# A trunk kernel whose last down projection streams 512 weight columns per matmul, with ten constant matmuls behind each post-norm sum

## What is computed

```
for i in range(DEPTH):
    y = swiglu(rms_norm(h, g[0]), ffn_w_gate[i, 0], ffn_w_up[i, 0], ffn_w_down[i, 0])
    h = h + 0.5 * rms_norm(y, g[1])
    u = rms_norm(h, g[2])
    y = mixer_ab(u, ...) if i % 2 == 0 else mixer_cd(u, ...)
    h = h + rms_norm(y, g[3])
    y = swiglu(rms_norm(h, g[4]), ffn_w_gate[i, 1], ffn_w_up[i, 1], ffn_w_down[i, 1])
    h = h + 0.5 * rms_norm(y, g[5])
return h[:, N_META:]
```

## Time and profile before

| | |
|---|---|
| median of three runs | 1197.17 us (1193.57 to 1197.82) |
| profiled execution | 1195.76 us |
| its span, first to last instruction | 1193.8 us |
| PE busy | 1138.9 us, 95% |
| DVE busy, ACT busy | 714.5 us, 547.3 us |
| mean granted TensorE clock | 0.978 |

### The profile page before, as it was taken

How to read it: one execution, slowest core, us unless ns; L and a number is a source line. 1 busy time by engine, 2 the same in 40 slices (tenths; PEclk the granted TensorE clock), 3 DMA queues, 4 the chain that set the end, 5 groups by cost and what they waited for, 6 DMA issues and landing times.

```text
span 1193.8 us, 20098 instructions
## 1 busy us (share of the span) xinstructions
PE 1138.9 (95%) x8979; PEld 1113.5 (93%) x8979; DVE 714.5 (60%) x753; ACT 547.3 (46%) x623; POOL 8.7 (1%) x12
## 2 busy tenths in 40 slices
PE   5999999899999899999999999999899699999997
PEld 5999999789999789999998999999899498999996
DVE  5565644668784676656446656554757636756542
ACT  5534343456633565343434544344463545444441
POOL 0000000000000000000000000000001100000000
PEclk9999999899999999999999999999999789999998
DMA  8656557677432145555563655455264024555530
GB/s 253 189 170 195 168 173 164 129 154 139 91 107 71 36 142 181 174 177 167 167 195 106 212 177 177 164 164 176 90 218 130 1 88 156 181 178 189 177 128 36
DMA packets 175780, 178.70 MB, mean 150 GB/s; under 512 B 4912, under 2 KB 174400, under 8 KB 175696
## 3 DMA queue, kind: packets, MB, share of 16 engines
q1 hardware_dynamic: 175696, 177.44, 49.8%
HBM read 176.38 MB, written 1.05 MB: 149 GB/s over the span
## 4 chain that ended last, share of the span: by engine, by line
PE 90%; DVE 5%; ACT 2%; DMA 2%; issue 1%; SPq 0%; DVEq 0%; ACTq 0%
PE ps L1531 24%; PE ps L1533 24%; PE ps L1532 24%; PE ps L1601 8%; PE ps L1568 2%; PE ps L1596 2%; PE ps L1569 2%; PE ps L1565 2%; DMA raw<-ab_w_in 1%; DVE w_lo L1018 1%; DVE hT L1067 1%; DVE yT L1066 1%; ACT w_hi L631 0%; DMA g_tok<-norm_gains 0%; PE ps L1588 0%
## 5 line engine op out<-in xcount | busy, mean ns | idle before, releaser
L1531 PE MATMUL ps<-u_hi,w_hi 128*128 128x272 f32 (+1 forms) x1696 | 491.3, 290 | 0.0
L1533 PE MATMUL ps<-u_hi,w_lo 128*128 128x272 f32 (+1 forms) x1696 | 487.9, 288 | 0.0
L1532 PE MATMUL ps<-u_lo,w_hi 128*128 128x272 f32 (+1 forms) x1696 | 486.0, 287 | 0.0
L1018 DVE TENSOR_TENSOR w_lo<-raw,w_hi 128x2048 fp32r<-128x2048 f32 (+1 forms) x169 | 378.0, 2259 | 123.3 <-ACT w_hi L631 123.3
L631 ACT ACTIVATE w_hi<-raw 128x2048 fp32r<-128x2048 f32 (+1 forms) x169 | 314.8, 1870 | 178.3 <-PE ps L1533 164.5
L1531 PEld LDWEIGHTS ps<-u_hi,w_hi 128*128 128x128 f32 x1696 | 319.5, 188 | 1.8 <-issue 0.8
L1532 PEld LDWEIGHTS ps<-u_lo,w_hi 128*128 128x128 f32 x1696 | 319.4, 188 | 0.3
L1533 PEld LDWEIGHTS ps<-u_hi,w_lo 128*128 128x128 f32 x1696 | 319.4, 188 | 0.0
L1531 PE MATMUL ps<-hid_hi,w_hi 128*128 128x272 f32 (+1 forms) x704 | 201.5, 286 | 0.0
L1533 PE MATMUL ps<-hid_hi,w_lo 128*128 128x272 f32 (+1 forms) x704 | 201.2, 286 | 0.0
L1532 PE MATMUL ps<-hid_lo,w_hi 128*128 128x272 f32 (+1 forms) x704 | 200.9, 285 | 0.0
(11 more groups left out here) (291 smaller groups left out, 939.6 us busy)
## 6 DMA issues: line engine op xcount, KB each, us to landing
raw<-ffn_w_gate SPq DMA_DIRECT2D x44, 1024.0 KB, 5.4
raw<-ffn_w_up SPq DMA_DIRECT2D x44, 1024.0 KB, 5.3
raw<-ffn_w_down SPq DMA_DIRECT2D x32, 896.0 KB, 4.6
raw<-ffn_w_down SPq DMA_DIRECT2D x16, 1024.0 KB, 5.0
raw<-ab_w_in SPq DMA_DIRECT2D x16, 1024.0 KB, 13.7
raw<-cd_w_in SPq DMA_DIRECT2D x9, 1024.0 KB, 5.4
raw<-ab_w_out SPq DMA_DIRECT2D x4, 1024.0 KB, 5.1
raw<-cd_w_out SPq DMA_DIRECT2D x4, 1024.0 KB, 5.1
```

Source lines behind the costliest of these rows:

```text
L1018: dve.tensor_tensor(dst, src, w_hi[:, n % NW, 0:rows(n) * CB].bitcast(F32), ALU.subtract)\
L1531: pe.matmul(o, wh, rhs_hi[:, kk, tok], start=first and kk == 0, stop=False)
L1532: pe.matmul(o, wh, rhs_lo[:, kk, tok], start=False, stop=False)
L1533: ins = pe.matmul(o, wl, rhs_hi[:, kk, tok], start=False, stop=last and kk == rows(n) - 1)
```

## The change

Two things are changed. First, behind `post_norm_sum` of every sub-layer but the last, PE runs ten float32 matmuls of `ones` against `ident`, 128 columns each, into a PSUM bank that nobody reads (`keep_clock`). They wait for nothing.

Second, the down projection of the last sub-layer is written anew (`last_down` on PE, ACT and DVE). The hidden activations become the stationary operand (128 tokens) and the weights the moving one, 512 columns at a time; there are two halves of 512 output features, each with six chunks of 4 or 3 rows (`LAST_ROWS`), and two tiles of 128 tokens, so 2 x 2 x 22 x 3 = 264 matmuls. The result is token-major. `hT` is transposed behind the first chunk and copied to `h_tok`. ACT squares a tile of the result with a sum along its free axis (`accum_out`), DVE adds the two sums of a token tile and multiplies the result by a row of gains (`g_row`, a new load of one row broadcast to 128 partitions), ACT makes the inverse root of one column, and DVE scales and adds `h_tok` in one instruction for each 512 columns. SP stores from `y_tok`, again in four pieces. The final post-norm, `make_input` and transposes of before are gone.

```diff
+LAST_ROWS = ((0, 4), (4, 8), (8, 12), (12, 16), (16, 19), (19, 22))
...
+                    if k == len(subs) - 1:
+                        sp.dma_start(g_row[:, :], a["norm_gains"][layer, norm_of(k) + 1:norm_of(k) + 2, :].to_broadcast([P, D]))\
+                            .then_inc(s_grow, 16)
+                        for z in range(2):
+                            for i, (k0, k1) in enumerate(LAST_ROWS):
+                                load(b + 2 * NPAIR + len(LAST_ROWS) * z + i, wd[:, k0:k1, z * BANK:(z + 1) * BANK], BANK)
+                        continue
...
+            def last_down(f, b):
+
+                n = b + 2 * NPAIR
+                for i in range(2):
+                    hi(n + i + 3)
+                for t in range(2):
+                    for z in range(2):
+                        act.wait_ge(s_hT, 2 * t + z + 1)
+                        act.activation(h_tok[:, t, z * BANK:(z + 1) * BANK], ps[:, 4 + 2 * t + z, :], ACT.Copy)\
+                            .then_inc(s_htok, 1)
+                for z in range(2):
+                    for i in range(len(LAST_ROWS)):
+                        if z or i > 1:
+                            hi(n + len(LAST_ROWS) * z + i + 3)
+                    for t in range(2):
+                        act.wait_ge(s_used, n + len(LAST_ROWS) * (z + 1)) if t else act.wait_ge(s_yt, z + 1)
+                        if z:
+                            act.wait_ge(s_yts, t + 1)
+                        act.activation(y_sq_tok[:, t, :], ps[:, 2 * z + t, :], ACT.Square, accum_out=y_sums[:, t, z:z + 1])\
+                            .then_inc(s_yts, 1)
+                        if z:
+                            act.wait_ge(s_ytot, t + 1)
+                            step.done(act.activation(y_root[:, t:t + 1], y_root[:, t:t + 1], ACT.Ln, bias=EPS, scale=1.0 / D))
+                            act.activation(y_root[:, t:t + 1], y_root[:, t:t + 1], ACT.Exp, bias=LN_HALF, scale=-0.5)\
+                                .then_inc(s_yroot, 1)
...
+            def last_down(f, b):
+
+                n = b + 2 * NPAIR
+                for z in range(2):
+                    cols = slice(z * BANK, (z + 1) * BANK)
+                    for i in range(len(LAST_ROWS)):
+                        lo(n + len(LAST_ROWS) * z + i + 3)
+                    if z == 0:
+                        dve.wait_ge(s_grow, 16)
+                        dve.wait_ge(s_htok, 4)
+                    for t in range(2):
+                        dve.wait_ge(s_yts, 2 * z + t + 1)
+                        if z:
+                            dve.tensor_tensor(y_root[:, t:t + 1], y_sums[:, t, 0:1], y_sums[:, t, 1:2], ALU.add).then_inc(s_ytot, 1)
+                        step.done(dve.tensor_tensor(y_tok[:, t, cols], ps[:, 2 * z + t, :], g_row[:, cols], ALU.mult))
+                        if z:
+                            dve.wait_ge(s_yroot, t + 1)
+                            for x in range(2):
+                                c_ = slice(x * BANK, (x + 1) * BANK)
+                                dve.scalar_tensor_tensor(y_tok[:, t, c_], y_tok[:, t, c_], y_root[:, t:t + 1], h_tok[:, t, c_],
+                                                         ALU.mult, ALU.add).then_inc(s_otok, 1)
...
+            def keep_clock(k):
+
+                bank = {"ffn": 3, "ab": 1, "cd": 3}[subs[k][0]]
+                for _ in range(10):
+                    pe.matmul(ps[:, bank, 0:P], ones[:, :], ident[:, :], start=True, stop=True)
...
+                for z in range(2):
+                    for i, (k0, k1) in enumerate(LAST_ROWS):
+                        n = b + 2 * NPAIR + len(LAST_ROWS) * z + i
+                        pe.wait_ge(s_lo, n + 1)
+                        pe.wait_ge(s_hid, 2 + NPAIR * f + (k1 + 1) // 2)
+                        for t in range(2):
+                            o, tok = ps[:, 2 * z + t, :], slice(N_META + t * P, N_META + (t + 1) * P)
+                            for kk in range(k0, k1):
+                                w = slice((kk - k0) * BANK, (kk - k0 + 1) * BANK)
+                                wh, wl = w_hi[:, n % NW, w], w_lo[:, n % NR, w]
+                                pe.matmul(o, hid_hi[:, kk, tok], wh, start=kk == 0, stop=False, skip_group_check=True)
+                                pe.matmul(o, hid_hi[:, kk, tok], wl, start=False, stop=False, skip_group_check=True)
+                                ins = pe.matmul(o, hid_lo[:, kk, tok], wh, start=False, stop=kk == KF - 1,
+                                                skip_group_check=True)
+                            if t == 0 and k1 == KF:
+                                ins.then_inc(s_yt, 1)
+                        ins.then_inc(s_used, 1)
...
                 post_norm_sum(k)
-
-            for g in range(2):
-                for t in range(2):
-                    pe.wait_ge(s_h, KD * len(subs) + 4 * g + 4)
-                    for m in range(4):
-                        src = hT[:, 4 * g + m, N_META + t * P:N_META + (t + 1) * P]
-                        ins = pe.transpose(ps[:, 2 + 2 * t + g, m * P:(m + 1) * P], src, ident[:, :])
-                    ins.then_inc(s_oT, 1)
+                keep_clock(k)
```

More of the change, by code:

```diff
@@ L310, in build @@
         s_dve = sem("dve_step")
-        s_oT = sem("output_transposed")
-        s_oa = sem("first_output_tile_copied")
-        s_oc = sem("second_output_tile_copied")
+        s_grow = sem("last_gain_row_loaded")
+        s_hT = sem("last_input_transposed")
+        s_htok = sem("last_input_copied")
+        s_yt = sem("last_y_ready")
+        s_yts = sem("last_y_squared")
+        s_ytot = sem("last_y_squares_added")
+        s_yroot = sem("last_y_root_ready")
+        s_otok = sem("output_ready")
         s_out = sem("output_stored")
@@ L472, in rows @@
                 if b <= n < b + SIZES[kind]:
+                    if b + SIZES[kind] == n_chunks and n - b >= 2 * NPAIR:
+                        k0, k1 = LAST_ROWS[(n - b - 2 * NPAIR) % len(LAST_ROWS)]
+                        return 2 * (k1 - k0)
                     if kind == "ffn" and n - b >= 2 * NPAIR:
@@ L525, in _, with load @@
             sp.dma_start(g_tok[:, :], a["norm_gains"].rearrange("l s (m p) -> (l s m) p", p=P)).then_inc(s_in, 16)
-            def load(n, src):
+            def load(n, src, cols=CB):
                 if n >= NR:
                     sp.wait_ge(s_used, n - NR + 1)
-                dst = raw[:, n % NR, 0:rows(n) * CB].rearrange("p (k c) -> p k c", c=CB)
+                dst = raw[:, n % NR, 0:rows(n) * CB].rearrange("p (k c) -> p k c", c=cols)
                 sp.dma_start(dst, src).then_inc(s_raw[n % NR], 16)
@@ L587, in _ @@
                         load(b + CD_CHUNKS + i, w_out[:, :, c0:c0 + CB])
-            for g in range(2):
[L590 to L593, removed]
+            for t in range(2):
+                for z in range(2):
+                    cols = slice(z * BANK, (z + 1) * BANK)
+                    sp.wait_ge(s_otok, 2 * t + z + 1)
+                    sp.dma_start(out[0, t * P:(t + 1) * P, cols], y_tok[:, t, cols]).then_inc(s_out, 16)
             sp.wait_ge(s_out, 64)
@@ L989, in _ @@
                     act.preload_act_table_set(EXP_SET)
+                    if k == len(subs) - 1:
+                        last_down(f, b)
+                        break
                     for blk in range(NBLK):
@@ L999, in _ @@
                 post_norm(k, kind)
-            for g in range(2):
-                act.wait_ge(s_oT, 2 * g + 1)
-                act.activation(o_tok[:, 0, g * BANK:(g + 1) * BANK], ps[:, 2 + g, :], ACT.Copy).then_inc(s_oa, 1)
         @block.vector
@@ L1084, in make_input @@
                         update_h(k, 2 * g + 2, 2 * g + 4)
[L1085 to L1088, removed]
+                    input_lo(k, layer, g)
                 for g in range(1, KD // 2):
@@ L1512, in _ @@
                     cd(k, b)
[L1513 to L1517, removed]
         @block.tensor
@@ L1598, in half_tile, with last_down @@
                 return ins
+            def last_down(f, b):
+                for z in range(2):
+                    for i, (k0, k1) in enumerate(LAST_ROWS):
+                        n = b + 2 * NPAIR + len(LAST_ROWS) * z + i
+                        pe.wait_ge(s_lo, n + 1)
+                        pe.wait_ge(s_hid, 2 + NPAIR * f + (k1 + 1) // 2)
+                        for t in range(2):
+                            o, tok = ps[:, 2 * z + t, :], slice(N_META + t * P, N_META + (t + 1) * P)
[9 more added lines that the diff above has]
+                        ins.then_inc(s_used, 1)
+                        if z == 0 and i == 0:
+                            pe.wait_ge(s_prod, 2 + NPAIR * f + NPAIR)
+                            for t in range(2):
+                                for g in range(2):
+                                    for m in range(4):
+                                        src = hT[:, 4 * g + m, N_META + t * P:N_META + (t + 1) * P]
```

(6 more changed lines are left out.)

10 lines of the change are left out of this document (7 added, 3 removed).

## The result

| | before | after |
|---|---|---|
| median of four runs each | 1196.79 us | 1183.65 us (1182.82 to 1184.62) |
| profiled execution, its span | 1195.76, 1193.8 us | 1184.62, 1182.7 us |
| mean granted clock | 0.978 | 0.983 |

The ratio after to before is 0.9895, with a 95% interval of 0.9874 to 0.9916: 13.1 us by the medians, and faster by more than the 0.5% that can be told. The forecast was 1185.0 us. The two profiled executions differ by 11.1 us; that of after was the slowest of its four runs.

What follows compares the result with a forecast made beforehand. PE bounds the kernel, busy 95% of the span. Clock -5.7, wider matmuls 0, transposes +1.75 and shorter end -7.6 sum to -11.5 us; forecast 1185.0 us, range 1180.5 to 1190.0.

Steps and rivals of the forecast that it cites:

- gap 3: Behind sub-layer 3, DVE and ACT set the pace, so keeping the clock there gains nothing.
- the fillers stay covered: Ten constant matmuls take 2.2 us at full clock and end before the next sub-layer's first matmul; 0.6 us cover left.
- the end of the program: From the last down matmul's end to the span's end: 5.7 us in place of 13.3, so -7.6 us.
- gap 0: Behind sub-layer 0 the ten run slowly and end 0.9 us late, 1.8 us are won back: 0.9 us gained.
- The worth of a fall: Behind sub-layers 1, 2 and 4, keeping full clock saves 1.6 us each, 4.8 us together.
- the wait for the third block of `u_hi`: At full clock PE uses up two blocks before the third comes, losing 0.1 us of the gain again.
- The width of a matmul: Last down projection: excess grows with columns, 512 take 0.2358 us, no gain from width; transposes add 1.75 us.
- the fixed-cost rival: Last down projection: 11.2 ns excess paid per matmul, so halving the matmuls gives 3.0 us more, 1182.0 us; chance 0.2.
- Constants that don't count: Rival: fillers behind the post-norm sums don't keep the clock, it falls as before; 1190.7 us, chance 0.13.
- The slow form of 512 columns: Rival: 512-column matmuls in the last down projection run at another rate; at 0.472 us each, 1247 us; chance 0.03.
- a supply that falls behind: Rival: last stage's weight chunks of other shape arrive late and PE waits up to 5 us; 1190 us, chance 0.04.
- The clock fell no later behind sub-layer 3: Rival: PE at full clock stands still more often between `u_hi` blocks, clock falls later; +1.7 us, 1186.7 us, no chance given.

## Why the prediction was right

**Point by point.** The time lies 1.3 us under the forecast and inside the range. That the clock is held behind 1 to 4, that gap 3 is worth nothing, that the fillers stay covered there (0.3 us of idleness is left in the timeline), and the end of the program, step by step, were right: the end is 5.6 us against 5.7, each step within 0.1 us. That the sum came so near is in part luck. Between the profiles the three falls gave 0.9 us less than forecast and gap 0 0.6 us less, and the last down projection cost 1.3 us less, so the errors nearly cancel; and the medians lie 13.1 us apart, the profiles 11.1.

**The worth of a fall was too high**, 1.6 us against 1.3. Two steps of that term failed. First, "they cost half their length" is not so. At half clock eight matmuls of 272 columns take 1.81 us, from the start at 643.97 to that of this one of the kernel before:

```profile
645.78 0.43 PE L1569 MATMUL ps<-u_hi,w_lo 128*128 128x272 f32 x1
```

That is 0.226 us each, just 272 columns at 1.2 GHz, while at full clock it is 0.1253 and not 0.113: the excess that a matmul has at full clock is not there at half. The ratio is 1.81, so a stretch of 3.4 us costs 1.5 us, not 1.7. The Trainium skill (TensorE: Matmul & The Clock Gate, Back-to-back issue gap) has the same form, N/1.2 with nothing added when cold; there the trace agrees. Second, the wait for the third block of `u_hi` costs 0.23 us where I had 0.1 us: from the last matmul of the second block to the second one of the third it is 0.48 us (643.00 to 643.48), where two starts in a dense stream are 0.25 us apart. 1.5 - 0.2 is the 1.3 that was measured three times.

**Gap 0 was right in kind and a little low**: the stretch was halved and the slow fillers delayed the next work by 0.8 us, as forecast (0.9). It was worth 0.9 us by the forecast and 1.0 to 1.35 us by comparing changed kernels with the same long fall at the end of ab (210.01 and 210.30 with fillers, 211.36 and 211.33 without). Against the profile of before only 0.3 us of it shows, because the execution profiled there had a shorter fall at the end of ab. The kernel with two fillers had the same pair of falls as before (6.8 us, then 3.4) and 210.55 us, against 210.57; with the long fall at the end of ab and no fillers it is 211.3 to 211.4, so that fall's length alone moves the part by 0.8 us. The prediction's reading that PE is busy all the time in these stretches, but for the one at 848 us, also fails behind sub-layer 0: 4.15 us of 6.70.

**The width of a matmul was half right.** I took the excess as growing with the columns, because the two sizes in the trace fit that. With a third size it is 11.2 ns at 256, 12.0 ns at 272 and 17.7 ns at 512 columns (231.0 - 213.3): neither fixed nor proportional. The stage (62.67 us) came out 1.3 us under my value (62.25 + 1.75 = 64.0) and 1.6 us over the fixed-cost rival (59.3 + 1.75 = 61.05). Its 264 matmuls cost 1.3 us less than the 528 of before, and the 16 transposes, 1.7 us here, ate that:

```profile
1119.99 1.91 PE L1694 MATMUL ps<-ident,hT 128*128 128x128 f32 x16
1121.65 0.48 PE L1681 MATMUL ps<-w_hi,hid_hi 128*128 128x512 f32 x1
```

The 215.8 ns that the prediction has for 512 columns by the Trainium skill's rule, as an estimate, were further off than either; the measurement decides, and it is 231 ns here.

**The rivals.** Constants that don't count are excluded by the fillers alone. The slow form of 512 columns did not come, nor did a supply that falls behind: within the stage PE waited for nothing. The clock fell no later behind sub-layer 3 (1.00 from 842.8 to 849.2 us). The rival that comes nearest is the fixed cost: of its 3.0 us 1.3 were real.

**What stays open.** Why two fillers, or none in one gap of one execution, are enough, and why a fall lasts 3.4 us in one place and 6.8 us in another, was not settled; the runs show only that behind 1 to 4 four do as well as ten. The parts add up to the 11.0 us between the spans of the two profiles. Of the 2 us by which the medians differ more, 1.0 lies with the changed kernel, whose profiled run was the slowest and had the lowest mean clock of the four (0.983; the others 0.984, 0.987 and 0.990 at 1183.97, 1183.34 and 1182.82 us); the other 1.0 lies in the scatter of the kernel before (1193.57 to 1197.82), which no run takes apart. What makes up the excess of a float32r matmul at full clock is open too.

## What to carry to other kernels

Look at the granted clock right behind each short stop of PE, not only at the stop: a stand of 2.4 us can cost 1.3 us more afterwards, and a few matmuls of constants that end before the awaited operand is there win it back for nothing. Count the fillers against the gap (what overruns is paid almost in full: 1.7 us too many cost 1.4 to 1.5 us a gap), and leave out the gaps behind which another engine sets the pace. Where the last matrix product feeds a chain of small steps, choose its orientation so that the result lies as it is stored and its norm is a sum along the free axis: that made the end 7.7 us shorter here, for 1.7 us of transposes; the wider matmul gave only 1.3.

## What the runs showed that I had not expected

At half clock a float32r matmul takes just its columns' time (0.226 us for 272), at full clock it has an excess of 11 to 18 ns (256 to 512 columns), so half clock costs 45% of a stretch and not 50%. Four float32 fillers, 0.9 us of work in a gap of 2.5 us, hold the clock behind sub-layers 1 to 4 as well as ten. A gap of 2.4 us without any left it at 1.00 once.
